# Sparse attention stage: results weighed by branch after the value product, and items turned two behind their scores

## The chip, the cores and the metric

One core of a Trainium2 chip runs the whole program. The metric is device time in microseconds (us). PE is TensorE (PEld its weight loads), DVE is VectorE, ACT is ScalarE, POOL is GpSimd, SP is SyncE, which here only issues DMAs.

## The reference

The program is one layer of a hybrid decoder for a prompt of 1024 tokens and a sample group of 8 sequences with 4 new tokens each and 4096 past tokens. The stage that is changed is the sparse attention (8 heads in 2 key/value groups of 4, head width 64). It computes three attentions per head over the same queries, and adds them with learned gates:

```python
def masked_softmax(s, mask):
    s = jnp.where(mask, s.astype(F32), -1e30)
    m = jnp.max(s, axis=-1, keepdims=True)
    e = jnp.exp(s - m) * mask
    return e / jnp.maximum(jnp.sum(e, axis=-1, keepdims=True), 1e-30)
...
o_c, o_s = nsa_cmp_slc(...)      # compressed blocks of 32 keys; selected blocks of 64 keys
o_w = nsa_window(...)            # the last 512 keys
gt = jax.nn.sigmoid(gl).reshape(Bh, Th, 3, NSA_KV, NSA_GQ, 1)
o = gt[:, :, 0] * o_c + gt[:, :, 1] * o_s + gt[:, :, 2] * o_w
```

The prompt has 16 blocks of 64 keys and 16 are selected, so for the prompt the selected branch is plain causal attention. For the sample group the selection matters, and its keys are gathered by pages of 128 tokens.

## The kernel before

The stage is the function `sparse`. It works through 50 items in one fixed order. 32 of them are prompt items: one of four head pairs (head r of group 0 and head r of group 1, written g = 0, 1) and one tile of 128 queries, tt = 0 to 7. The first head pair takes its tiles in the order 0, 7, 1, 6, 2, 5, 3, 4, the others in the order 0 to 7. From the fifth prompt item on, 18 set items stand between them: a set is one chunk of 512 past keys (4 pages) for 4 sequences of the sample group, 16 of the selected branch and 2 of the window.

A prompt item has a row of scores per query and g: 128(tt+1) columns of the selected branch (SLC), then 128 min(tt+1, 5) of the window (WIN), then 4(tt+1) compressed ones (CMP). It goes through these steps, one after the other, while other items are in the other steps:

- `score` (L1763, PE): the row in chunks of 512 columns, into one of two pairs of PSUM banks (`score_bank`). A chunk waits until DVE has read the chunk two before it (semaphore `biased`).
- `biases` (L2054 to L2061, DVE): adds the bias, writes the row to `s_` (`nsa_probs`, four slots) and takes maxima; from them the negative maxima, which release the exponentials (`negm_ready`).
- `exps` (L1911, ACT): six exponentials in place, one per g and branch, each with its sum.
- `scales` (L2071 to L2080, DVE): from the sums and the gates one factor per query, g and branch, in three small instructions; then six instructions that multiply the row by them.
- `turn` (L1784, PE): transposes blocks of 128 keys, two blocks with both g to a group of one PSUM bank, the compressed keys as a last group. Two such banks are in turn.
- `copies` (L1931, ACT): copies each group to `pt` (`nsa_probs_t`, three slots).
- `values` (L1810, PE): multiplies with the values, two groups behind the turning. All groups of an item add up in one 128 x 128 region of bank 6 or 7.
- `keep_result` (L1949, ACT): copies the region to the output tile.

A set item goes the same way with one chunk (L1752, L2007, L1904), one or two groups (L1777, L1799) and no scaling of its row. The sum of its chunks is formed at the end (L2105, L2108) on DVE.

Each engine's program is written out by hand in steps. In step i PE scores item i and turns item i - LAG, with LAG = 3, chunks of scores and pairs of groups spread evenly among each other (`merged`). ACT in step i copies the groups of item i - 3 and puts one of the six exponentials of item i - 1 before the first and one behind each copy; those that are left come at the end of the step. DVE in step i does `biases(i)` and then `scales(i - 1)`, which has to wait for ACT's last exponential of that item. All engines are in order, so what stands behind a waiting instruction waits as well. In steps 1 and 3 DVE also ranks the blocks of the sample group (`compare`, `count`), and in step 6 it makes masks from the ranks.

SP issues the loads of queries and biases of a head pair (`load`, L1711 and L1714) and of 9 of 16 pages of each set, POOL those of the other 7 (L1702). A set's buffer is free when the values of the set three before it are done. The load of head pair r waits until the last result of head pair r - 2 has been copied out (`o_out`).

Of the kernel before, what the change touches and what calls it, by code (L numbers as in the profile page):

```python
# [13 lines left out]
ALU = mybir.AluOpType  # L14
ACT = mybir.ActivationFunctionType
AX_X = mybir.AxisListType.X
F32 = mybir.dt.float32
# [1527 lines left out]
def sparse(nc, t, u, kv, toeplitz, ident, by_token, out, gdn, spill, kvp, space, pages, kct, vc_past, past_space, early):  # L1545
# [13 lines left out]
    SLOTS, TSLOTS, TBANKS, REGIONS, LAG = 4, 3, 2, 2, 3  # L1559
    PROMPT, SET = range(2)  # L1560
    PAGES, NEWKEYS = "pages", "new"
# [40 lines left out]
    first_chunk, first_group = [0], [0]  # L1602
    for i in range(NI):
        first_chunk.append(first_chunk[-1] + n_chunks(i))
        first_group.append(first_group[-1] + len(groups(i)))
    BEHIND = 2
# [7 lines left out]
    with ExitStack() as ctx:  # L1614
# [12 lines left out]
        assert next_place(nc) - ranking_at >= 3 * 16 * PAGE * 2 and early.end - early.at >= 16 * PAGE * 2  # L1627
# [5 lines left out]
        cnt, flag, addm, near = S("count", [P, IH]), S("flag", [P, NBLK]), S("block_mask", [P, 2, NBLK]), S("near", [P, 2, PAGE])  # L1633
        oc, acc = S("set_out", [P, 2, 2, P]), S("sample_sum", [P, 2, P])
# [4 lines left out]
        def alias(name, shape):  # L1639
# [5 lines left out]
        ring = alias("ring", [P, 2, HB, 4, 2 * PAGE])  # L1645
        third = nc.alloc_sbuf_tensor_at("nsa_ring_third", [P, HB - 1, 4, 2 * PAGE], F32, offset=ranking_at)
        third_last = nc.alloc_sbuf_tensor_at("nsa_ring_third_last", [P, 4, 2 * PAGE], F32, offset=early.at)
# [9 lines left out]
        region = lambda i: ps[:, O_BANK + i % REGIONS, 0:P]  # L1657
        sem = phase_semaphores(ctx, nc, "nsa_")
# [5 lines left out]
        (scores_mm, biased, cleared, max_ready, negm_ready, exp_ready, chain, probs_ready, pt_mm, pt_out, pv_mm, o_mm, o_out) = (  # L1664
            sem(s) for s in ("scores_mm", "biased", "cleared", "max_ready", "negm_ready", "exp_ready", "chain", "probs_ready",
                             "pt_mm", "pt_out", "pv_mm", "o_mm", "o_out"))
# [71 lines left out]
        def _(pe):  # L1738
# [3 lines left out]
            def score(i, c):  # L1742
                kind, n, tt = items[i]
                G = first_chunk[i] + c
# [42 lines left out]
            def values(i, k):  # L1787
# [16 lines left out]
                else:  # L1804
                    for j, (x, col, vb) in enumerate(group):
                        w = 4 * (tt + 1) if x == CMP else P
                        for g in range(2):
# [61 lines left out]
            for i in range(NI + LAG):  # L1869
# [11 lines left out]
                tailing = [(i - LAG, s) for s in range(0, len(groups(i - LAG)), 2)] if i >= LAG else []  # L1881
                for which, (n, k) in merged(scoring, tailing):
                    if which:
# [3 lines left out]
                        values_up_to(first_group[n] + pair[-1] + 1 - BEHIND)  # L1887
                    else:
                        score(n, k)
            values_up_to(first_group[NI])  # L1890
            for hf in range(2):
                pe.wait_ge(sum_ready, hf + 1)
                pe.wait_ge(biased, first_chunk[NI])
# [3 lines left out]
        def _(act):  # L1897
# [43 lines left out]
            def keep_result(i):  # L1941
                kind, n, tt = items[i]
                act.wait_ge(o_mm, i + 1)
                if kind == SET:
                    x, hf, c = sets[n]
                    dst = oc_set[:, hf, c, :] if x == SLC else oc[:, hf, 0, :]
                else:
                    dst = out[:, n, tt * P:(tt + 1) * P]
                act.activation(dst, region(i), ACT.Copy).then_inc(o_out, 1)  # L1949
# [48 lines left out]
        def _(dve):  # L1998
# [13 lines left out]
            def set_biases(i):  # L2012
                x, hf, c = sets[items[i][1]]
                G, dst = first_chunk[i], s_[:, i % SLOTS, 0, :]
# [12 lines left out]
                add_biases(stat_of(items[i][1]), pieces, (biased, first_chunk[i + 1])).then_inc(negm_ready, 1)  # L2027

            def biases(i):
# [12 lines left out]
                for c, pieces in enumerate(chunks(tt)):  # L2042
                    G = first_chunk[i] + c
# [13 lines left out]
                dve.wait_ge(biased, first_chunk[i + 1])  # L2057
# [5 lines left out]
            def scales(i):  # L2063
# [8 lines left out]
                dve.wait_ge(chain, 3 * n + 2)  # L2072
                V.reciprocal(scale[:, p, :, :], scale[:, p, :, :]).then_inc(chain, 1)
                dve.wait_ge(chain, 3 * n + 3)
# [87 lines left out]
            def masks():  # L2162
                dve.wait_ge(spread_mm, 1)
                for hf in range(2):
# [12 lines left out]
            for i in range(NI + 1):  # L2177
# [4 lines left out]
                if i >= 1:  # L2182
                    scales(i - 1)
# [1012 lines left out]
```

## Time and profile before

| | us |
|---|---|
| median of 3 runs (2793.57 to 2802.07) | 2799.81 |
| the profiled execution | 2800.31 |
| its span, first to last instruction | 2798.6 |
| of it the item loop of the sparse stage, 1073.0 to 1440.2 | 367.2 |
| in this stretch: PE busy / DVE busy / ACT busy | 313.1 / 223.4 / 229.3 |

In the whole span PE is busy for 2621.9 us (94%), DVE for 1318.0, ACT for 853.8. The stage stands in slices 16 to 21 of 40, and in them PE has 8s where most other slices have 9s. The stages before and after it do not overlap with it: the first load of the next stage is issued at 1442.64 us and its first matmul starts at 1448.60 us. Times below are from the span's start.

### The profile page before, as it was taken

To read this page: it belongs to the slowest core of one execution; us is meant where nothing else is said; L and a number is where in the kernel's file an instruction comes from. 1 tells how busy PE (TensorE), PEld (TensorE's weight loads), DVE (VectorE), ACT (ScalarE), POOL (GpSimd) and SP (SyncE) were. 2 spreads that over 40 slices of the span, in tenths; PEclk is the share of its full clock that TensorE was granted. 3 is DMA by queue.
4 is the path that set the end of the run, shared out by engine and by line. 5 is a ranking of instruction groups with operands and counts; after the bars stand their busy time and mean duration, and the time that the engine had idled before them with its cause. 6 is when DMAs were issued, how large, how long until landed. Compare 5 with 4: busy or idle time off the path is not lost. (4 is left out here: it accounts for less than half of the span.)

```text
span 2798.6 us, 52706 instructions
## 1 busy us (share of the span) xinstructions
PE 2621.9 (94%) x21842; PEld 2422.9 (87%) x21842; DVE 1318.0 (47%) x2314; ACT 853.8 (31%) x1606; POOL 701.9 (25%) x554
## 2 busy tenths in 40 slices
PE   8999999999889887898879999999999999999997
PEld 7999999999867774555559999988999999999996
DVE  6989999313134357456543453234333323224233
ACT  5323111113123334665642132144221121120222
POOL 2222222222144331212104325201522222222222
PEclk9999999999969898999989999999999999999998
DMA  5122352332287636434335441243111111111111
GB/s 187 46 69 56 105 105 87 93 92 77 95 268 228 205 105 238 150 118 148 104 112 177 137 172 54 68 166 114 46 46 46 46 46 46 46 46 46 46 46 70
DMA packets 149345, 290.33 MB, mean 104 GB/s; under 512 B 28356, under 2 KB 97160, under 8 KB 146354
## 3 DMA queue, kind: packets, MB, share of 16 engines
q1 hardware_dynamic: 137586, 255.49, 28.8%
q0 software_dynamic: 11520, 31.47, 3.6%
q8 instruction: 173, 2.83, 0.4%
q14 instruction: 66, 0.54, 0.1%
HBM read 245.94 MB, written 51.93 MB: 106 GB/s over the span
## 5 line engine op out<-in xcount | busy, mean ns | idle before, releaser
L147 POOL TENSOR_TENSOR mlp_w_low<-mlp_w_raw,mlp_w_high 128x1024 fp32r<-128x1024 f32 x72 | 173.6, 2411 | 649.4 <-ACT mlp_w_high L143 649.4
L373 PE MATMUL in_psum<-x_high,in_w_high 128*128 128x352 f32 x1416 | 265.9, 329 | 21.7 <-DVE x_low L568 11.7
L147 POOL TENSOR_TENSOR in_w_low<-in_w_raw,in_w_high 128x1024 fp32r<-128x1024 f32 x59 | 146.9, 2490 | 547.3 <-ACT in_w_high L143 547.3
L143 ACT ACTIVATE mlp_w_high<-mlp_w_raw 128x1024 fp32r<-128x1024 f32 x72 | 76.4, 1061 | 621.5 <-PE mlp_psum L2850 621.5
L2850 PE MATMUL mlp_psum<-mlp_in,mlp_w_high 128*128 128x352 f32 x1536 | 264.9, 324 | 0.0
L373 PEld LDWEIGHTS in_psum<-x_high,in_w_high 128*128 128x128 f32 x1416 | 236.5, 191 | 29.9 <-issue 15.4
L373 PE MATMUL in_psum<-x_low,in_w_high 128*128 128x352 f32 x1416 | 261.3, 326 | 0.0
L373 PE MATMUL in_psum<-x_high,in_w_low 128*128 128x352 f32 x1416 | 258.7, 324 | 0.0
L2850 PEld LDWEIGHTS mlp_psum<-mlp_in,mlp_w_high 128*128 128x128 f32 x1536 | 251.2, 189 | 0.2
L373 PEld LDWEIGHTS in_psum<-x_low,in_w_high 128*128 128x128 f32 x1416 | 237.4, 191 | 0.0
L373 PEld LDWEIGHTS in_psum<-x_high,in_w_low 128*128 128x128 f32 x1416 | 234.6, 189 | 0.0
L2618 PE MATMUL mix_psum<-branch_halves,mix_w_high 128*128 128x352 f32 x960 | 179.3, 327 | 11.9 <-DVE branch_halves L2703 8.6
L527 DVE SCALAR_TENSOR_TENSOR branches<-glu_prompt,conv_a_taps,branches 128x1024 f32<-128x1024 f32 x120 | 189.6, 1580 | 0.0
L147 POOL TENSOR_TENSOR mix_w_low<-mix_w_raw,mix_w_high 128x1024 fp32r<-128x1024 f32 (+1 forms) x56 | 109.8, 1962 | 306.1 <-ACT mix_w_high L143 306.1
L2850 PE MATMUL mlp_psum<-hidden_high,mlp_w_high 128*128 128x352 f32 x960 | 178.0, 324 | 1.8 <-PEq L86 1.8
L2850 PE MATMUL mlp_psum<-hidden_high,mlp_w_low 128*128 128x352 f32 x960 | 177.8, 324 | 0.0
L2850 PE MATMUL mlp_psum<-hidden_low,mlp_w_high 128*128 128x352 f32 x960 | 177.8, 324 | 0.0
L143 ACT ACTIVATE in_w_high<-in_w_raw 128x1024 fp32r<-128x1024 f32 x59 | 62.4, 1057 | 366.1 <-PE in_psum L373 350.2
L2618 PEld LDWEIGHTS mix_psum<-branch_halves,mix_w_high 128*128 128x128 f32 x960 | 161.0, 191 | 12.6 <-issue 12.4
L2850 PEld LDWEIGHTS mlp_psum<-hidden_high,mlp_w_high 128*128 128x128 f32 x960 | 159.0, 189 | 2.0 <-issue 2.0
L2850 PEld LDWEIGHTS mlp_psum<-hidden_high,mlp_w_low 128*128 128x128 f32 x960 | 159.2, 189 | 0.0
L2850 PEld LDWEIGHTS mlp_psum<-hidden_low,mlp_w_high 128*128 128x128 f32 x960 | 159.0, 189 | 0.0
(493 smaller groups left out, 4429.8 us busy)
## 6 DMA issues: line engine op xcount, KB each, us to landing
mlp_w_raw<-in_w_mlp SPq DMA_DIRECT2D x64, 512.0 KB, 3.6
in_w_raw<-in_w_in SPq DMA_DIRECT2D x59, 512.0 KB, 4.2
gdnp_page_ring<-in_cache_cmp POOLq DMA_DIRECT2D x128, 128.0 KB, 4.8
gdnp_page_ring<-in_cache_cmp SPq DMA_DIRECT2D x128, 128.0 KB, 4.9
u_scratch<-stage SPq DMA_DIRECT2D x28, 528.0 KB, 5.2
aux<-u_scratch SPq DMA_DIRECT2D x24, 528.0 KB, 4.0
nsa_ring<-in_cache_slc SPq DMA_DIRECT2D x90, 128.0 KB, 4.0
nsa_ring<-in_cache_slc POOLq DMA_DIRECT2D x70, 128.0 KB, 4.1
```

What stands on the lines that cost most here:

```text
L143: act.activation(self.high[:, i % 2, 0:k * P], self.raw[:, i % 2, 0:k * P], ACT.Copy).then_inc(self.rounded, 1)
L147: self.nc.gpsimd.tensor_tensor(self.low[:, i % 2, 0:k * P], self.raw[:, i % 2, 0:k * P], self.high[:, i % 2, 0:k * P].bitcast(F32), ALU.su ...
L373: return mm(psum[:, e % 2, n, 0:WN], w[:, i % 2, c * P:(c + 1) * P], a[:, c, n * WN:(n + 1) * WN], start=x == 0 and c == 0, stop=x == 2 an ...
L527: V.scalar_tensor_tensor(out=y, in0=src, scalar=w, in1=y, op0=ALU.mult, op1=ALU.add).then_inc(conv_chain, 1)
L2618: return mm(psum[:, e % 2, n, 0:cols.stop - cols.start], w[:, i % 2, c * P:(c + 1) * P], a(c)[:, cols], start=x == 0 and c == 0, stop=x == ...
L2850: return mm(psum[:, e % 2, n, 0:WN], w[:, i % 2, c * P:(c + 1) * P], a(c)[:, column(n)], start=x == 0 and c == 0, stop=x == 2 and c == CHU ...
```

## The change

The row of exponentials is no longer multiplied. The values are multiplied with the bare exponentials, each branch into a region of its own (three of 128 columns in the same bank). The three factors per query and g are brought into the layout of the result by six small matmuls per prompt item (`factors`: the factor column, repeated 64 times, as weights, against the identity), which take the place of one chunk in the score banks. ACT copies all three regions (384 columns in place of 128) to `weighed`; DVE multiplies them with the factors and adds the three (`combine`). DVE computes the factors three steps after the item's biases instead of one, and combines in the fourth step after. LAG is 2 in place of 3, so PE turns and ACT copies an item one step sooner; turning waits for the exponentials alone. The load of head pair r waits for the maxima of the last item of head pair r - 2 (`negm_ready`) instead of its result. To find room, some small tiles of the sample group (`near`, `addm`, `acc`) lie in memory that is free by then, and the masks wait for the end of one early store (`spilled`).

```diff
-    SLOTS, TSLOTS, TBANKS, REGIONS, LAG = 4, 3, 2, 2, 3
+    SLOTS, TSLOTS, TBANKS, REGIONS, LAG = 4, 3, 2, 2, 2
...
-    first_chunk, first_group = [0], [0]
+    of_step = lambda step: step - LAG - 2
+    STEPS = NI + LAG + 2
+    combined = lambda step: of_step(step) >= 0 and items[of_step(step)][0] == PROMPT
+    chunk_at, factors_at, n_all_chunks, first_group = [], {}, 0, [0]
+    for step in range(STEPS):
+        chunk_at.append(n_all_chunks)
+        n_all_chunks += n_chunks(step) if step < NI else 0
+        if combined(step):
+            factors_at[step] = n_all_chunks
+            n_all_chunks += 1
...
-    BEHIND = 2
+    BEHIND, BEFORE_SCALES = 2, 3
...
+        by_branch = lambda i: ps[:, O_BANK + i % REGIONS, 0:3 * P].rearrange("p (x n) -> p x n", x=3)
...
                 if r >= 2:
-                    sp.wait_ge(o_out, last_of_head[r - 2] + 1)
+                    sp.wait_ge(negm_ready, last_of_head[r - 2] + 1)
...
+            def factors(step):
+                G, n = factors_at[step], prompts_before[of_step(step)]
+                if G >= 2:
+                    pe.wait_ge(biased, G - 1)
+                pe.wait_ge(scale_ready, n + 1)
+                for x in range(3):
+                    for g in range(2):
+                        last = mm(score_bank(G, 0)[g * DH:(g + 1) * DH, x * P:(x + 1) * P],
+                                  scale[:, n % SLOTS, g, x:x + 1].to_broadcast([P, DH]), ident[:, :], start=True, stop=True)
+                last.then_inc(scores_mm, 1)
...
                 if k == 0:
-                    pe.wait_ge(*((probs_ready, prompts_before[i + 1]) if kind == PROMPT else (exp_ready, i + 1)))
+                    pe.wait_ge(exp_ready, i + 1)
...
-                            last = mm(region(i)[dims, :], v, pt[0:w, G % TSLOTS, 2 * j + g, :], start=k == 0 and j == 0, stop=x == CMP)
+                            last = mm(by_branch(i)[dims, x, :], v, pt[0:w, G % TSLOTS, 2 * j + g, :], start=vb == first_block,
+                                      stop=x == CMP or vb == tt)
...
                 scoring = [(i, c) for c in range(n_chunks(i))] if i < NI else []
-                tailing = [(i - LAG, s) for s in range(0, len(groups(i - LAG)), 2)] if i >= LAG else []
+                if i in factors_at:
+                    scoring.append((i, FACTORS))
+                tailing = [(i - LAG, s) for s in range(0, len(groups(i - LAG)), 2)] if LAG <= i < NI + LAG else []
+                if i == NI + LAG:
+                    values_up_to(first_group[NI])
...
-                    dst = out[:, n, tt * P:(tt + 1) * P]
-                act.activation(dst, region(i), ACT.Copy).then_inc(o_out, 1)
+                before = prompts_before[i]
+                if before >= 2:
+                    act.wait_ge(prompt_out, before - 1)
+                act.activation(weighed[:, before % 2, :, :], by_branch(i), ACT.Copy).then_inc(o_out, 1)
...
-                V.tensor_tensor(scale[:, p, :, :], scale[:, p, :, :], gate, ALU.mult).then_inc(chain, 1)
-                dve.wait_ge(chain, 3 * n + 4)
-                for g in range(2):
-                    for x, at, w in spans(tt):
-                        src = s_[:, i % SLOTS, g, at:at + w]
-                        last = V.tensor_scalar(src, src, scale[:, p, g, x:x + 1], None, ALU.mult)
-                last.then_inc(probs_ready, 1)
+                V.tensor_tensor(scale[:, p, :, :], scale[:, p, :, :], gate, ALU.mult).then_inc(scale_ready, 1)
+
+            def combine(step):
+                m = of_step(step)
+                kind, r, tt = items[m]
+                G, n = factors_at[step], prompts_before[m]
+                dve.wait_ge(scores_mm, G + 1)
+                dve.wait_ge(o_out, m + 1)
+                rows = weighed[:, n % 2, :, :]
+                V.tensor_tensor(rows, rows, score_bank(G, 0)[:, 0:3 * P].rearrange("p (x n) -> p x n", x=3), ALU.mult).then_inc(biased, 1)
+                dve.wait_ge(biased, G + 1)
+                V.tensor_reduce(out[:, r, tt * P:(tt + 1) * P], rows.rearrange("p x n -> p n x"), AX_X, ALU.add
+                                ).then_inc(prompt_out, 1)
...
             def masks():
                 dve.wait_ge(spread_mm, 1)
+                dve.wait_ge(spilled, 16)
...
-            for i in range(NI + 1):
+            for i in range(STEPS):
                 if i == RANKED:
                     masks()
                 if i < NI:
                     biases(i)
-                if i >= 1:
-                    scales(i - 1)
+                if BEFORE_SCALES <= i < NI + BEFORE_SCALES:
+                    scales(i - BEFORE_SCALES)
+                if i in factors_at:
+                    combine(i)
```

## Rows read from the trace of the kernel before

**Rows 1.** Busy time and PEclk by stretch: the item loop, then two shorter stretches.
```profile
core 0: us, PE busy (x) PEld busy (x) DVE busy (x) ACT busy (x) POOL busy (x), PEclk, DMA share, GB/s
1073.00:1440.20 367.20, 313.07 (x3115) 202.04 (x3115) 223.35 (x1035) 229.33 (x666) 61.13 (x112) 0.93 0.39 128
1265.00:1275.00 10.00, 6.41 (x54) 4.12 (x52) 6.64 (x39) 2.86 (x10) 0.00 (x0) 0.68 0.58 206
1320.00:1335.00 15.00, 12.96 (x140) 8.38 (x136) 9.66 (x38) 10.31 (x27) 4.12 (x7) 1.00 0.44 142
```

**Rows 2.** Waits in the item loop: us in total, times, longest.
```profile
PE nsa_psum L1763 <- DVE nsa_part_max L2054: 34.0, 22, 8.7
PE nsa_psum L1784 <- ACT nsa_probs_t L1931: 6.9, 14, 1.1
PE nsa_psum L1752 <- DMA nsa_ring_third<-in_cache_slc: 6.6, 1, 6.6
PE nsa_psum L1784 <- DVE nsa_probs L2080: 5.5, 7, 2.0
...
DVE nsa_scale L2071 <- ACT nsa_probs L1911: 34.3, 20, 3.5
...
ACT nsa_probs L1911 <- DVE nsa_negmax L2061: 63.7, 27, 6.4
```

**Rows 3.** Timeline around one stall: start, duration, instruction, idle before it.
```profile
1300.36 0.17 DVE L2071 TENSOR_SCALAR nsa_scale<-nsa_sums 128x6 f32<-128x6 f32 x1 [2.83 <-ACT nsa_probs L1911]
...
1301.00 2.23 DVE L2080 TENSOR_SCALAR nsa_probs<-nsa_probs,nsa_scale 128x640 f32<-128x640 f32 x6
...
1304.49 0.92 PE L1763 MATMUL nsa_psum<-nsa_k_prompt,nsa_q_heads 64*128 64x384 f32 x4 [1.99 <-DVE nsa_part_max L2054]
...
1307.43 0.94 ACT L1911 ACTIVATE nsa_probs<-nsa_probs,nsa_negmax 128x768 f32<-128x768 f32 x1 [4.88 <-DVE nsa_negmax L2061]
```

**Rows 4.** Groups by line, the stage: form, count, busy us, mean ns, idle before.
```profile
L2080 DVE TENSOR_SCALAR nsa_probs<-nsa_probs,nsa_scale 128x640 f32<-128x640 f32 (+11 forms) x192 | 64.1, 406 | 1.1
L1810 PE MATMUL nsa_psum<-nsa_probs_t,nsa_v_by_token 128*64 128x128 f32 x1056 | 78.7, 284 | 0.0
L1949 ACT ACTIVATE branches<-nsa_psum 128x128 f32<-128x128 f32 x32 | 8.4, 264 | 1.1 <-PE nsa_psum L1810 0.9
```

**Rows 5.** PE in the timeline at full clock: scores, transposes, values, a set's scores.
```profile
1412.35 1.13 PE L1763 MATMUL nsa_psum<-nsa_k_prompt,nsa_q_heads 64*128 64x512 f32 x4
1434.24 1.09 PE L1810 MATMUL nsa_psum<-nsa_probs_t,nsa_v_by_token 128*64 128x128 f32 x16
1431.22 1.09 PE L1784 MATMUL nsa_psum<-ident,nsa_probs 128*128 128x128 f32 x8
1259.72 1.06 PE L1752 MATMUL nsa_psum<-nsa_ring,early_q_padded 128*32 128x512 f32 x8
```

**Rows 6.** Groups by line with shapes kept apart: the nearest forms to what is added.
```profile
L2007 DVE CUSTOM_DVE_ANT_1 nsa_probs<-nsa_psum,nsa_block_mask 128x384 f32<-128x384 f32 x2 | 1.1, 554 | 2.2 <-PE nsa_psum L1752 2.2
L1931 ACT ACTIVATE nsa_probs_t<-nsa_psum 128x512 f32<-128x512 f32 x146 | 86.0, 591 | 59.4 <-PE nsa_psum L1784 38.6 <-PE nsa_psum L1777 9.8 <-PE nsa_psum L1810 7.6
L1931 ACT ACTIVATE nsa_probs_t<-nsa_psum 128x256 f32<-128x256 f32 x8 | 3.1, 383 | 2.2 <-PE nsa_psum L1784 1.7 <-PE nsa_psum L1810 0.3
```

**Rows 7.** Timeline of the loop's start: exponentials of item 1, a reduction, PE's return.
```profile
1080.67 1.15 ACT L1911 ACTIVATE nsa_probs<-nsa_probs,nsa_negmax 128x1024 f32<-128x1024 f32 x1 [2.70 <-DVE nsa_negmax L2061]
...
1082.19 0.28 DVE L2146 TENSOR_REDUCE nsa_score<-nsa_psum 128x64 f32<-128x128 f32 x1
...
1085.09 0.19 ACT L1911 ACTIVATION_READ_ACCUMULATOR nsa_probs<-nsa_probs,nsa_negmax 128x1 f32 x1
...
1089.53 3.78 PE L1763 MATMUL nsa_psum<-nsa_k_prompt,nsa_q_heads 64*128 64x512 f32 x12 [8.70 <-DVE nsa_part_max L2054]
```

**Rows 8.** Timeline: SP's queue at the load of a head pair.
```profile
1170.33 0.33 SPq L1711 DMA_DIRECT2D nsa_q_heads<-u_scratch  x1
```

**Rows 9.** Timeline of the loop's end: ACT's last copies.
```profile
1440.00 1.61 ACT L1994 ACTIVATE branches<-nsa_psum 64x16 f32<-64x16 f32 x16
```

More of the change, by code:

```diff
@@ L1558, in sparse @@
     CMP, SLC, WIN = range(3)
-    SLOTS, TSLOTS, TBANKS, REGIONS, LAG = 4, 3, 2, 2, 3
+    SLOTS, TSLOTS, TBANKS, REGIONS, LAG = 4, 3, 2, 2, 2
     PROMPT, SET = range(2)
-    PAGES, NEWKEYS = "pages", "new"
+    PAGES, NEWKEYS, FACTORS = "pages", "new", "factors"
     sets = [(x, hf, c) for hf in range(2) for x, c in [(WIN, 0)] + [(SLC, c) for c in range(NCH)]]
@@ L1626, in sparse @@
         lower, gtm, eqm = (sb(ctx, nc, "nsa_" + n, [P, IH, NBLK], dt) for n, dt in (("lower", U16), ("greater", BF16), ("equal", BF16)))
-        assert next_place(nc) - ranking_at >= 3 * 16 * PAGE * 2 and early.end - early.at >= 16 * PAGE * 2
+        assert next_place(nc) - ranking_at >= 3 * 16 * PAGE * 2 + 8 * NBLK and early.end - early.at >= 16 * PAGE * 2
         gates24, gates = S("gates24", [P, 2, 3, NSA_HEADS]), S("gates", [P, 2, 3])
@@ L1632, in sparse @@
         inv, score, scol = S("inv", [P, 2]), S("score", [P, NBLK]), S("score_col", [P, IH])
-        cnt, flag, addm, near = S("count", [P, IH]), S("flag", [P, NBLK]), S("block_mask", [P, 2, NBLK]), S("near", [P, 2, PAGE])
-        oc, acc = S("set_out", [P, 2, 2, P]), S("sample_sum", [P, 2, P])
+        cnt, flag = S("count", [P, IH]), S("flag", [P, NBLK])
+        oc, weighed = S("set_out", [P, 2, 2, P]), S("weighed", [P, 2, 3, P])
+        assert NCMP == P
+        acc = sc
         least, weight, total, coef = S("least", [P, 2]), S("weight", [P, 2, NCH]), S("total", [P, 2, NCH + 4]), S("coef", [P, 2, NCH + 2])
@@ L1645, in sparse @@
         ring = alias("ring", [P, 2, HB, 4, 2 * PAGE])
+        near = alias("near", [P, 2, PAGE])
+        assert place[0] <= space + 2 * 4 * 4 * W
         third = nc.alloc_sbuf_tensor_at("nsa_ring_third", [P, HB - 1, 4, 2 * PAGE], F32, offset=ranking_at)
+        addm = nc.alloc_sbuf_tensor_at("nsa_block_mask", [P, 2, NBLK], F32, offset=ranking_at + 3 * 16 * PAGE * 2)
         third_last = nc.alloc_sbuf_tensor_at("nsa_ring_third_last", [P, 4, 2 * PAGE], F32, offset=early.at)
@@ L1663, in sparse @@
             "k_in", "v_turned", "v_ready", "vc_turned", "vc_ready", "spilled"))
-        (scores_mm, biased, cleared, max_ready, negm_ready, exp_ready, chain, probs_ready, pt_mm, pt_out, pv_mm, o_mm, o_out) = (
-            sem(s) for s in ("scores_mm", "biased", "cleared", "max_ready", "negm_ready", "exp_ready", "chain", "probs_ready",
-                             "pt_mm", "pt_out", "pv_mm", "o_mm", "o_out"))
+        (scores_mm, biased, cleared, max_ready, negm_ready, exp_ready, chain, scale_ready, pt_mm, pt_out, pv_mm, o_mm, o_out, prompt_out) = (
+            sem(s) for s in ("scores_mm", "biased", "cleared", "max_ready", "negm_ready", "exp_ready", "chain", "scale_ready",
+                             "pt_mm", "pt_out", "pv_mm", "o_mm", "o_out", "prompt_out"))
         (lower_in, zeroed, bias_mm, bias_ready, m0_mm, m0_read, turned_mm, turned, past_mm,
@@ L1743, in score @@
                 kind, n, tt = items[i]
-                G = first_chunk[i] + c
+                G = chunk_at[i] + c
                 if G >= 2:
@@ L1806, in values @@
                         w = 4 * (tt + 1) if x == CMP else P
+                        first_block = {SLC: 0, WIN: max(0, tt - 4), CMP: 0}[x]
                         for g in range(2):
@@ L1868, in _ @@
             pe.wait_ge(k_in, 32)
-            for i in range(NI + LAG):
+            for i in range(STEPS):
                 if i == LAG:
@@ L1887, in _ @@
                         values_up_to(first_group[n] + pair[-1] + 1 - BEHIND)
+                    elif k == FACTORS:
+                        factors(n)
                     else:
                         score(n, k)
-            values_up_to(first_group[NI])
             for hf in range(2):
                 pe.wait_ge(sum_ready, hf + 1)
-                pe.wait_ge(biased, first_chunk[NI])
+                pe.wait_ge(biased, n_all_chunks)
                 tr(ps[:, hf, 0:P], acc[:, hf, :], ident[:, :]).then_inc(final_mm, 1)
@@ L2026, in set_biases @@
                         pieces += [(dst[:, at:BANK], src[:, at:BANK], near[:, hf, :]), new(1)]
-                add_biases(stat_of(items[i][1]), pieces, (biased, first_chunk[i + 1])).then_inc(negm_ready, 1)
+                add_biases(stat_of(items[i][1]), pieces, (biased, chunk_at[i] + 1)).then_inc(negm_ready, 1)
             def biases(i):
@@ L2176, in _ @@
             dve.wait_ge(chain, 1)
-            for i in range(NI + 1):
+            for i in range(STEPS):
                 if i == RANKED:
```

15 lines of the change are left out of this document (7 added, 8 removed).

## The prediction, made before the changed kernel was run

> **What bounds the kernel now.** I read the waits first, then stretches of the stage, then one stall in the timeline. The item loop lasts 367.2 us; PE is busy for 313.1 of them, DVE for 223.4 and ACT for 229.3 [rows 1]. So PE is the fullest engine, but it stands for 54.1 us, and it also works slowly at times: the mean granted clock is 0.93, which is 313.1 x 0.07 = 22 us of its busy time. What does it wait for? 34.0 us for DVE's reading of a score bank, 5.5 for DVE's scaling of a row, 6.9 for ACT's copies of turned groups, 6.6 once for a page load [rows 2]. DVE is no full engine either. It stands for 34.3 us until ACT has done an item's last exponential, and ACT stands for 63.7 us until DVE has the next item's negative maxima [rows 2]. That is a ring: `scales(i - 1)` waits for the exponentials of i - 1, `biases(i + 1)` stands behind it on DVE, PE's score chunks and ACT's next exponentials wait for that. One turn of it in the timeline [rows 3]: DVE stands 2.83 us for ACT, multiplies for 2.23 us, reads banks again, PE comes back after 1.99 us of idling and ACT after 4.88. The clock follows such stalls: in 1265 to 1275, with PE busy for 6.41 of 10 us, it is 0.68, so for much of the stretch the engine ran at 1.2 GHz instead of 2.4; in 1320 to 1335, busy for 12.96 of 15 us with many small gaps, it is 1.00 [rows 1].
>
> **The change part by part.**
>
> 1. Six multiplications per prompt item go from DVE: 192 instructions, 64.1 us [rows 4]. The three small instructions before them stay, but two steps later, when the exponentials are long done, so DVE's 34.3 us of waiting goes with them.
>
> 2. DVE gets two instructions per prompt item. The product reads 384 columns from PSUM: the nearest row is a bias addition of that size from PSUM, 554 ns [rows 6]. The sum reads 384 and writes 128 columns, in steps of 128 columns. The nearest row is a reduction of 128 columns, 0.28 us; at about 1.05 ns per column (0.55 - 0.28 us over 256 columns) 384 columns make 0.55 us [rows 6, 7]. From both sides: 0.28 us if its size cost nothing, 1.1 us if the stride doubled it. Together 32 x 1.1 = 35 us. DVE's load falls from 223 to about 194 us of the loop, and the 29 us are worth nothing by themselves, since DVE isn't the fullest engine. If the stride cost double, DVE would still be at 212.
>
> 3. PE gets six matmuls per prompt item, on the path. Their shape is that of the value products: weights 128 x 64, 128 columns moving, the two g in different halves of the array. The trace records each value product twice (528 products, 1056 records), and 16 records take 1.03 us from one group's start to the next one's [rows 4, 5]. 12 records are 0.77 us, over 32 items **25 us**. Below: 0.27 us less per item if the weights, one repeated column, loaded free (about 16 us in all). Above: 50 us if the two g didn't run side by side. I take 25, since the form is the row's own.
>
> 4. ACT's copy of a result grows from 128 to 384 columns: from 264 ns to a value between 383 (256 columns) and 591 (512), about 487 [rows 4, 6]. 32 x 0.22 = 7 us, beside PE's work; ACT then has about 236 of the loop.
>
> 5. The ring is cut, so PE's 34.0 + 5.5 us lose their cause. What is late next? With LAG = 2 PE turns item i - 2 in step i, and ACT did its exponentials in step i - 1, at that step's end where the copies beside them are few. To size it I wrote down, for each step, what each engine has to do. PE: 0.25 us + 2.2 ns per column of score width, 0.54 us per block of 128 keys (four records of 64 ns for its two value products, two transposes of 136 ns) and once more for the compressed keys, 0.17 us per group; a set 1.1 + 1.9 us [rows 5]. ACT: per exponential 0.27 us + 0.86 ns per column (1.15 us for 1024 columns, 4.6 for the six of item 1 [rows 7]), 0.6 us per full group, the result. DVE: 0.09 us + 1.04 ns per column, and the small instructions. For the kernel before, with LAG = 3, these sums give PE 326, ACT 243 and DVE 223 us, close to the trace. If each step lasts as long as its fullest engine, the loop is 363 us, that is 37 over PE's sum; measured are 54.1 - 6.6 (the load) = 47.5 of idling. For the kernel after they give PE 350, ACT 250, DVE 191 and 370 in all, 20 over PE's sum: 7 in steps 0 and 1, where DVE ranks, and 13 in ten steps where ACT is the fullest, most of them with a set's single group. An example is step 24: ACT copies a set's group and does the six exponentials of a tile with tt = 7 (4.6 + 0.9 us), while PE has the scores of a tile with tt = 0, the set's tail, and no factors (0.8 + 1.9 us). Scaled with what the sums missed before, 20 x 47.5 / 37 = **25 us** of idling after.
>
> 6. The start. PE stands for 8.70 us until 1089.53, while DVE ranks [rows 7]. With LAG = 2 it can turn item 0 in step 2; item 1 it can turn once its exponentials end at about 1085.3 [rows 7]. This is part of the 25 us.
>
> 7. Loads. PE waited 6.6 us for pages of the third buffer [rows 2]; SP had issued a head pair's load at 1170.33, just ahead of them [rows 8]. A set's buffer comes free one step (some 7 us) sooner, and the head pair's load may go four steps sooner, so I count this wait as gone; if it stays, 6.6 us come back. On SP's queue the load keeps its place in the order, and the page loads behind it wait for later values anyway. POOL's queue loses nothing.
>
> 8. The clock. Before, 22 us go to slow stretches, and they follow the longer stalls [rows 1]. With idling about halved I halve this: 12 us. The range is 5 to 22.
>
> 9. The end. Two more of the small tails: PE does the last two items' factors (counted), ACT's last copy is 0.22 us longer, and DVE's 1.1 us run beside the 1.61 us of ACT's last copies [rows 9]. 0.5 us. The new waits of `masks` for a store and of ACT for `prompt_out` are for work done steps before; I see nothing to be late there, and cost them at nothing. If the second were late, copies would stand behind it and PE would show it as waits for `nsa_probs_t`.
>
> The sum: 313.1 - 22 = 291 us of PE's work at full clock, + 25 (factors), + 25 (idling), + 12 (clock), + 0.5 = 353.5, against 367.2: 13.7 us less. All other stages keep their time, since the next one starts its loads only when this one is over. The profiled execution took 2800.3 us, which is 0.5 above the median of the runs; 2800.3 - 13.7 = **2786.6 us**.
>
> **A rule that speaks against step 8.** In the item loop PE had many gaps under 1 us with the clock at 1.00, as in 1320 to 1335 [rows 1]. The Trainium skill, page "TensorE: Matmul & The Clock Gate", section "A second HAM failure mode: psum-queue depth-cycling", says that frequent short gaps between groups of matmuls, as banks are cycled, are enough to make the clock swing. By that rule the changed loop, with more and shorter waits, keeps its 22 us. The trace disagrees so far.
>
> **The rivals.**
>
> *Clock and waits stay (same time).* The gaps are shared out differently, but the clock loss stays at 22 us and idling falls only to 36 (the sums' 20 + the 16 by which measured idling exceeds them at the start and in ping-pong between PE and ACT). 291 + 25 + 36 + 22 = 374 is 7 over; with either alone it is 363 to 364, about 4 less. So 2796 to 2807, centre 2800. For it: ACT's share rises and its copies already cost PE 6.9 us [rows 2]. Against: DVE's 34 us have no other cause than the ring. A clock that alone stays as it was gives the 363.
>
> *The exponentials are late (slower).* Place: the first `turn` of a step. 30 of 50 items are followed into it by an item with four groups or fewer (18 sets, 12 tiles with tt up to 2), where ACT has up to four of six exponentials left behind its last copy: two thirds of 4.6 us for the widest. PE covers this with its last two groups of values, the factors and one score chunk, together up to 1.1 + 0.8 + 1.1 us [rows 5]. It decides from the point where the exponentials left over take longer than that cover. If the cover is mostly only the values, about 1.6 us are lost each time, 48 us, and with the clock at its old loss: 291 + 25 + 22 + 48 = 386, that is 19 over, 2819 us.
>
> *The factors cost double (slower).* If the repeated column as weights keeps the two g from running side by side, 25 more: 2812 us. It would show at once in the group of the new line.
>
> *More is gained (faster).* If idling falls to 15 us and the clock loss to 5, the loop is 336 and the time 2769. For it: PE can be nearly gapless, 14.6 of 15 us, where nothing but turning and values is left; but that is without scores, so I give it little.
>
> *The change doesn't do what it says*, that is, DVE still waits for ACT or PE in `combine`: the factors stand last in a step, and DVE waits for them with the next `biases` behind it. But those need scores that PE issues later still, so this wait costs nothing by itself.
>
> **How the numbers follow.** Forecast (2779 to 2796) 0.48; same 0.20; exponentials late 0.12; factors double 0.06; more gained 0.14. The predicted time is the forecast's, 2787. The range 2768 to 2811 takes in the forecast, the same, the gain and most of the doubled factors, and leaves out the late exponentials and the tails. What a measurement of this kernel can tell from no change is about 0.3%, 8.4 us, so faster means under 2791.4: 0.36 of the forecast's 0.48 and the 0.14, together 0.50. Same: the remaining 0.12 and 0.19 of the same, 0.31. Slower: 0.19.
>
> **What would show it right or wrong.** Right: the group of the multiplications is gone; DVE's wait for ACT is near 0 and PE's for DVE's reading is under 10 us, most of it at the start; the new matmuls come to about 25 us in 384 records; PE's wait for pages is gone; PEclk in the loop is 0.96 or more. Wrong: transposes that wait for `nsa_probs` of ACT for more than 20 us (exponentials late), a new line's group near 50 us (factors), a clock that stays at 0.93.

## The result, and the profile after

The changed kernel takes 2805.95 us (median of 20 runs, 2794.79 to 2813.06), the kernel before, measured beside it, 2795.9 us (20 runs). The ratio is 1.0031, with a 95% interval of 1.0021 to 1.0040: it is slower by 0.3%, at the edge of what can be told from no change. The prediction was 2787 us, faster. The time lies within the range, on the wrong side of no change.

The same view as [rows 1], for the item loop of the kernel after, cut at two instructions, its first score matmul and PE's last transpose:

```profile
core 0: us, PE busy (x) PEld busy (x) DVE busy (x) ACT busy (x) POOL busy (x), PEclk, DMA share, GB/s
1081.32:1450.69 369.37, 330.82 (x3499) 225.40 (x3498) 197.23 (x907) 241.66 (x664) 60.31 (x112) 0.94 0.38 124
```

The loop of the kernel before, cut at the same two instructions:

```profile
1073.20:1440.07 366.87, 312.87 (x3115) 201.97 (x3114) 223.35 (x1035) 229.20 (x664) 61.13 (x112) 0.93 0.39 128
```

The waits of the kernel after, as in [rows 2] (engine, tile and line, what it waited for: us in total, times, longest):

```profile
DVE nsa_weighed L2118 <- PE nsa_psum L1788: 39.1, 24, 6.2
...
PE nsa_psum L1809 <- ACT nsa_probs L1943: 27.6, 19, 3.5
...
PE nsa_psum L1777 <- DVE nsa_part_max L2088: 3.7, 3, 2.8
...
PE nsa_psum L1788 <- DVE nsa_part_max L2088: 2.1, 1, 2.1
PE nsa_psum L1777 <- DVE nsa_score L2186: 2.0, 1, 2.0
```

The new groups, as in [rows 4, 6]:

```profile
L1788 PE MATMUL nsa_psum<-ident,nsa_scale 128*64 128x128 f32 x384 | 26.6, 275 | 2.1 <-DVE nsa_part_max L2088 2.1
...
L2120 DVE TENSOR_REDUCE branches<-nsa_weighed 128x128 f32<-128x384 f32 x32 | 19.0, 594 | 1.1
L2118 DVE TENSOR_TENSOR nsa_weighed<-nsa_weighed,nsa_psum 128x384 f32<-128x384 f32 x32 | 17.7, 554 | 44.4 <-PE nsa_psum L1788 39.1 <-issue 5.1
L1983 ACT ACTIVATE nsa_weighed<-nsa_psum 128x384 f32<-128x384 f32 x32 | 15.4, 483 | 3.7 <-PE nsa_psum L1836 3.7
```

The reader should see three things. The ring of [rows 2, 3] is gone: DVE no longer waits for an exponential, PE's 34.0 us for the reading of a bank before its scores are 3.7 (and 2.1 before the factors), and the wait for pages isn't there. A new wait has come: 19 times PE stands before a transpose (L1809) until ACT has done the exponentials (L1943), 27.6 us. And PEclk is 0.94, where 0.96 or more was expected.

The profiled run of after took 2810.4 us, and most of its difference from before's profiled run lies ahead of the loop: the loop started at 1081.32 instead of 1073.20, and stages ahead of it, which the change doesn't touch, had a lower granted clock in that execution. A second profile, below, has no such difference. So parts are compared here by the length of the loop.

### The profile page after: what moved, and what is told of

It reads as the page before. It is cut to its first block and busy times, and to the rows that moved or that the text cites. A ratio compares the mean times of both kernels' runs of the same rounds, so it can differ in the third digit from the quotient of the medians.

```text
span 2808.7 us, 53440 instructions
## 1 busy us (share of the span) xinstructions
PE 2648.5 (94%) x22226; PEld 2453.9 (87%) x22226; DVE 1293.6 (46%) x2186; ACT 867.0 (31%) x1606; POOL 702.3 (25%) x554
## 5 line engine op out<-in xcount | busy, mean ns | idle before, releaser
L373 PE MATMUL in_psum<-x_high,in_w_high 128*128 128x352 f32 x1416 | 265.9, 329 | 21.9 <-DVE x_low L568 11.9
L2661 PEld LDWEIGHTS mix_psum<-branch_halves,mix_w_high 128*128 128x128 f32 x960 | 160.7, 191 | 12.4 <-issue 12.2
```

The source lines that it names most:

```text
L373: return mm(psum[:, e % 2, n, 0:WN], w[:, i % 2, c * P:(c + 1) * P], a[:, c, n * WN:(n + 1) * WN], start=x == 0 and c == 0, stop=x == 2 an ...
L2661: return mm(psum[:, e % 2, n, 0:cols.stop - cols.start], w[:, i % 2, c * P:(c + 1) * P], a(c)[:, cols], start=x == 0 and c == 0, stop=x == ...
```

## The experiments

Each loop was cut at the same instructions. From its row I work out three shares: idling is its length less PE's busy time, the clock's part is busy time x (1 - PEclk), and work at full clock is the rest. PEclk has two digits, so the last two shares are good to about 1.7 us. Each row is one profiled execution; the ratio is that of the timed runs, by their medians. All in us, but for the ratio:

| kernel | loop | idling | clock | work | ratio to before, 95% interval |
|---|---|---|---|---|---|
| before | 366.9 | 54.0 | 21.9 | 291.0 | |
| after, first profile | 369.4 | 38.6 | 19.8 | 311.0 | 1.0031 [1.0021, 1.0040] |
| after, second profile | 374.1 | 38.8 | 23.5 | 311.8 | 1.0033 [1.0021, 1.0045] |
| after with LAG 3 | 337.8 | 19.8 | 9.5 | 308.4 | 0.9901 [0.9886, 0.9916] |
| after, exponentials first | 346.8 | 27.7 | 6.4 | 312.7 | 0.9955 [0.9940, 0.9969] |
| LAG 3, exponentials first | 336.0 | 22.1 | 3.1 | 310.8 | 0.9901 [0.9879, 0.9922] |
| LAG 3, one third of the factors | 326.3 | 24.2 | 6.0 | 296.1 | 0.9862 [0.9841, 0.9884] |
| LAG 3, factors twice | 355.9 | 17.7 | 6.8 | 331.5 | 0.9960 [0.9944, 0.9977] |
| LAG 3, the old load | 345.9 | 26.1 | 9.6 | 310.2 | 0.9919 [0.9889, 0.9949] |
| before with LAG 2 | 472.7 | 121.9 | 63.1 | 287.7 | 1.0389 [1.0366, 1.0412] |
| before, factors an item later | 431.5 | 92.5 | 47.5 | 291.5 | 1.0242 [1.0228, 1.0256] |
| before, factors ahead of the biases | 367.5 | 51.1 | 25.3 | 291.1 | 0.9995 [0.9979, 1.0010] |

**The changed kernel again.** No edit.

> The changed kernel once more, unaltered, for a second profile. In the first one the item loop took 369.6 us (before: 367.2), while the stages ahead of it had taken 5.3 us more and the prelude of the sparse stage 2.8 us more, both at a lower granted clock. Theory A (these 8 us are what the clock does from run to run, and the loop's 2 to 3 us are the change): the loop again takes 367 to 372 us, and the time ahead of the loop differs from 1081 us, towards 1073. Rival (the change reaches the stages ahead of it, through where tiles or code lie): the loop starts again at 1080 us or later.

2805.94 us. The loop starts at 1072.16, close to before's 1073.20, and lasts 374.1 us:

```profile
1072.16:1446.26 374.10, 335.27 (x3498) 227.75 (x3498) 197.41 (x907) 241.86 (x664) 60.11 (x112) 0.93 0.38 126
```

So the later start of the first profile was not the change. The loss inside the loop is 7.2 us here and 2.5 in the first profile. The wait for exponentials is the same to 0.1 us (27.6, 19 times, longest 3.5). What differs between the two profiles is mostly the clock: 3.7 of the 4.7 us.

**LAG 3 again.** Of the change the weighing by branch and the earlier load of the head pairs stay, so this is not the weighing alone, as the expectation calls it.

```diff
-    SLOTS, TSLOTS, TBANKS, REGIONS, LAG = 4, 3, 2, 2, 2
+    SLOTS, TSLOTS, TBANKS, REGIONS, LAG = 4, 3, 2, 2, 3
```

> The changed kernel with LAG = 3, so items are turned three behind their scores as before, and only the weighing by branch is left of the change. Theory A (the 27.6 us that PE waits for ACT's exponentials come from turning an item sooner; the 26.6 us of factor matmuls stay): that wait falls under 3 us, the loop to 367.2 + 26.6 - (34.0 + 5.5 + most of the 6.6) - some clock = 345 to 352 us, and the time to 2778 to 2785 us. Rival B (ACT's copies and exponentials hold PE up whatever the lag; the waits turn up as waits for nsa_probs_t or for banks): the loop stays within 3 us of 369.6 and the time at 2800 to 2806.

2768.51 us, more than was expected, and better than both kernels. Its loop row:

```profile
1072.58:1410.33 337.75, 317.95 (x3499) 215.17 (x3498) 195.97 (x907) 235.44 (x665) 60.11 (x112) 0.97 0.42 137
```

The same stretch in two parts, split after the first 37 us:

```profile
1072.58:1109.58 37.00, 27.24 (x211) 17.31 (x210) 28.78 (x120) 21.39 (x68) 7.55 (x14) 0.82 0.74 254
1109.58:1410.33 300.75, 290.71 (x3292) 197.87 (x3288) 167.19 (x787) 214.05 (x599) 52.56 (x98) 0.99 0.38 123
```

The largest waits of PE in it (L1777 is the scores, L1788 the factors, L1809 the turning):

```profile
PE nsa_psum L1777 <- DVE nsa_part_max L2088: 10.0, 6, 7.0
PE nsa_psum L1809 <- ACT nsa_probs_t L1963: 5.8, 11, 1.4
PE nsa_psum L1788 <- DVE nsa_part_max L2088: 1.6, 4, 0.4
```

Turned three items behind, no transpose waits for an exponential. After the first 37 us PE idles for 10.0 of 300.75 us. Against before the loop is 29.1 us shorter: 34.2 less idling and 12.4 less to the clock, for 17.4 more work. LAG 2 then takes 36.3 back (second profile): 19.0 of idling, 14.0 of clock, and 3.4 of work, which is within what two digits of PEclk allow. The change is two changes of opposite sign.

**The exponentials ahead of the copies** (after, LAG 2). ACT puts as many of the six before its first copy as would be left behind the last one.

```diff
-                next(exp_parts, None)
+                for _ in range(max(1, 6 - len(groups(i)))):
+                    next(exp_parts, None)
```

> The changed kernel, LAG = 2, with ACT's order altered in steps with fewer than five groups: the exponentials that were left behind the last copy are done ahead of the first one. Theory A says that PE's 27.6 us are these leftovers: the wait for them halves at least (under 14 us), the loop falls by 5 to 15 us to 355 to 365. Rival B: the copies are late instead and PE waits as long for nsa_probs_t or its values; the loop stays at 366 to 372 us.

2782.22 us. The wait falls from 27.6 to 10.7 us, the loop by 27.3 against the second profile, of which 11.1 are idling and 17.1 the clock. Its loop row:

```profile
1072.14:1418.93 346.79, 319.05 (x3499) 217.48 (x3498) 197.26 (x907) 238.91 (x665) 60.11 (x112) 0.98 0.42 134
```

And what is left of PE's wait:

```profile
PE nsa_psum L1809 <- ACT nsa_probs L1943: 10.7, 10, 2.9
PE nsa_psum L1809 <- ACT nsa_probs_t L1964: 5.8, 8, 1.4
```

The second line is new: with copies standing behind exponentials, 5.8 us of the 16.9 come back as waits for copies, which is why idling falls by 11.1 only. The loops behind their first 37 us, of the second profile of the changed kernel and then of this one:

```profile
1109.16:1446.26 337.10, 306.45 (x3278) 208.97 (x3274) 168.86 (x793) 219.25 (x598) 52.80 (x99) 0.93 0.35 112
1109.14:1418.93 309.79, 290.24 (x3278) 198.66 (x3274) 168.80 (x793) 216.02 (x596) 52.57 (x99) 0.99 0.39 122
```

Nothing but ACT's order was changed, so the late exponentials are shown as the cause of the waits, and the clock's loss goes with them. The profiled execution was the fastest of six (2778.05 us); by the medians the gain is 23.7 us and not 27, so the typical clock loss is some us above the 6.4 of the table.

**The same order with LAG 3.** Both edits.

> by_branch_lag3 with the order of exponentials of exps_first. With LAG = 3 no one waits for the exponentials any more. Theory A: no gain, the loop stays at 337.8 +- 3 us and the time at 2766 to 2771. Rival B (ACT's order also delays copies with LAG = 3, and the 5.8 us that PE waits for nsa_probs_t go up): 341 us or more.

2768.94 us, no different from LAG 3 alone. Where the exponentials have a step to spare, their place costs nothing.

**Before with LAG 2.**

```diff
-    SLOTS, TSLOTS, TBANKS, REGIONS, LAG = 4, 3, 2, 2, 3
+    SLOTS, TSLOTS, TBANKS, REGIONS, LAG = 4, 3, 2, 2, 2
```

> The kernel before with LAG = 2 and nothing else: the other half of the change alone. Theory A (turning an item sooner has no slack for the steps between scores and turning; here these are the exponentials and also DVE's multiplications): PE waits for nsa_probs of DVE or ACT for far more than the 27.6 us of the changed kernel, 40 to 80 us, and the loop of 367 us grows to 395 to 430, the time to 2825 to 2860. Rival B (the lag by itself costs little, and only the two together meet): the loop stays under 380 us.

2906.61 us, far worse than I thought: with the row still to be multiplied, exponentials, factors and products all have to be done in the slack that is left. PE's largest wait, for the multiplied rows (L2080):

```profile
PE nsa_psum L1784 <- DVE nsa_probs L2080: 113.8, 28, 7.7
```

So the rest of the change, without which LAG 2 costs 3.9%, brings it to 0.3%, but doesn't make it free.

**Before, with the factors an item later.** DVE multiplies the row of item i - 2 behind the biases of item i.

```diff
-                if i >= 1:
-                    scales(i - 1)
+                if i >= 2:
+                    scales(i - 2)
```

> The kernel before, with the whole row still multiplied on DVE, but one step later: scales(i - 2) behind biases(i). No factor matmuls, LAG = 3. Theory A (the ring between DVE and ACT was the whole of the stall, and it can be cut without any work on PE): DVE's wait of 34.3 us for the exponentials falls under 8 us, PE's 34.0 us for score banks under 15, the loop to 335 to 350 us and the time to 2768 to 2783. Rival B: PE's first turn of a step now waits for the multiplications, which end after the biases of that step; 50 steps x 1 us or more come back as waits for nsa_probs of DVE, the loop stays at 360 us or more.

2866.46 us, a miss. The wait of DVE for exponentials goes from 34.3 to 1.0 us, as meant, but the multiplied rows now come late for PE:

```profile
PE nsa_psum L1784 <- DVE nsa_probs L2080: 77.6, 29, 5.1
```

At this place the multiplication cuts the ring and misses another due time, that of the turning. No other place was tried that differs from the kernel before (the next experiment does not), so what is shown is that taking it out of the row's path pays and this move doesn't.

**Before, with the factors ahead of the biases.** The same call, put ahead of `biases(i)`.

> The kernel before with the row multiplied on DVE at the start of the next step: scales(i - 2) ahead of biases(i) instead of scales(i - 1) behind biases(i). scales_later (behind biases(i)) had cut DVE's wait for the exponentials to 1.0 us, but PE waited 77.6 us for the multiplied rows and the loop took 431 us. Theory A (with LAG = 3 there is one step for it: done first, the rows are ready when PE turns them; DVE waits a little for the last exponentials, PE a little for banks): loop 345 to 365 us. Rival B (DVE's multiplications stand between the scores of a step and the maxima that ACT waits for, wherever they are put, so the ring is there again): 365 us or more, with PE's wait for score banks at 30 us or more.

2795.01 us, no difference. The experiment was badly chosen: biases i, factors i - 1, biases i + 1 is the very order of the kernel before, only cut into steps elsewhere. DVE waits for exponentials for 29.9 us (18 times), PE for the reading for 30.8. It says nothing on either theory, except that the place of the ranking beside these calls doesn't matter.

**A third of the factor matmuls** (LAG 3).

```diff
-                for x in range(3):
+                for x in range(1):
```

> by_branch_lag3 with two of the six factor matmuls per item (one branch of three), 128 in place of 384 records; the product then reads what lies in the banks for the other two branches, so the prompt's attention result isn't computed fully. It prices the matmuls on PE's path. Theory A (PE is the engine that sets the pace, and each record costs its 64 to 70 ns): the loop falls by two thirds of 26.6, 17 to 18 us, from 337.8 to about 320, the time from 2768.5 to 2750 to 2753. Rival B (the matmuls lie partly in gaps of PE): it falls by less than 9 us.

2758.85 us. The kernel leaves out the factors of two of the three branches, so it serves as a price only. PE works 15.8 us less and the loop is 11.4 shorter (9.7 by the medians), between the two expectations: 72% of the time taken away counts. The rest turns into idling (24.2 in place of 19.8).

**The factor matmuls twice** (LAG 3).

```diff
-                for x in range(3):
+                for x in (0, 1, 2, 0, 1, 2):
```

> As by_branch_lag3, with the six factor matmuls issued twice per prompt item (12; the second six write the same values again). The attention result is complete. by_branch_lag3 had 2768.5 us, a loop of 337.8 and 26.6 us in the factor matmuls; with two of six left it had 9.7 us less for 15.8 us less of PE work. Theory A, the matmuls lie on the path where PE is the fullest engine and in PE's idle time elsewhere, so some 65 to 90% of their time counts: the added 26 us make the loop 17 to 25 us longer (355 to 363), 2785 to 2794 us, and PE's busy time in the loop rises to about 343. Rival B, they are fully on the path, or worse (the first bank's clock loss grows): 26 us or more, 2795 or above. Rival C, mostly hidden beside the chunk's waits: under 12 us, below 2781.

2789.32 us. PE works 20.3 us more, the loop is 18.2 longer: 90%. Little of the added work finds cover. The group of the factors' line in this kernel:

```profile
L1788 PE MATMUL nsa_psum<-ident,nsa_scale 128*64 128x128 f32 x768 | 48.8, 278 | 1.7 <-DVE nsa_part_max L2088 1.6
```

And with the plain LAG 3, so that twice the matmuls take 21.2 us more, 0.66 per item:

```profile
L1788 PE MATMUL nsa_psum<-ident,nsa_scale 128*64 128x128 f32 x384 | 27.6, 281 | 1.7 <-DVE nsa_part_max L2088 1.6
```

**The old load** (LAG 3).

```diff
-                    sp.wait_ge(negm_ready, last_of_head[r - 2] + 1)
+                    sp.wait_ge(o_out, last_of_head[r - 2] + 1)
```

> As by_branch_lag3, with the load of head pair r waiting again for the last result of head pair r - 2, as in the kernel before, in place of its maxima. It prices that part of the change. Theory A: the head pair's load is issued some four steps later, and the page loads that stand behind it in SP's queue with it, so a wait of PE for pages comes back, once, of 3 to 8 us, and the time is 2771 to 2777. Rival B: the page loads wait for their buffers anyway and nothing in the time changes, 2767 to 2770, with the set's scores waiting under 1 us for pages.

2777.34 us; the loop is 8.2 us longer, and by the two ratios the difference is 5 us (0.0018 x 2797), with intervals that overlap. The wait of [rows 2] is back in its old place:

```profile
PE nsa_psum L1766 <- DMA nsa_ring_third<-in_cache_slc: 6.3, 1, 6.3
```

What SP waited for, with the old load and then with the new one:

```profile
SPq L1725 <- ACT nsa_weighed L1983: 16.1, 1, 16.1
SPq L1716 <- PE nsa_psum L1824: 10.3, 1, 10.3
```

SP's queue in the timeline, with the old load:

```profile
1171.13 0.33 SPq L1725 DMA_DIRECT2D nsa_q_heads<-u_scratch  x1
...
1177.08 1.39 SPq L1716 DMA_DIRECT2D nsa_ring_third<-in_cache_slc  x3
```

The same with the new load:

```profile
1153.57 0.43 SPq L1725 DMA_DIRECT2D nsa_q_heads<-u_scratch  x1
...
1170.30 1.39 SPq L1716 DMA_DIRECT2D nsa_ring_third<-in_cache_slc  x3
```

With the old load SP stood for 16.1 us until ACT had copied a result (L1983), and the page loads stood behind it. With the new one SP gets to them in time and waits only for their buffer (L1824, 10.3 us). The pages are issued 97.7 us after the loop's start in place of 103.4.

## Why the prediction was wrong, step by step

Predicted for the loop were 316 us of PE's work at full clock with the factors, 25 of idling, 12 of clock and 0.5 at the end. Measured in the first profile were 311.0, 38.6 and 19.8. So 13.6 us were missed in idling and 7.8 in the clock, and 5.5 were counted too much in work and the end: together 15.9, which is 369.4 - 353.5. In the second profile the loop is 20.6 us over the forecast. By the medians of the runs 13.7 us less were forecast and 10.1 more came.

1. *The multiplications and DVE's wait*: right. Both are gone.
2. *DVE's two instructions*: right, 554 + 594 ns for 0.55 + 0.55 us. The sum, with its stride, takes 594 ns, near the 0.55 said and far from 1.1. DVE is busy for 197 us (194 said). Its 39.1 us of waiting for the factors' matmuls in `combine` cost nothing that shows: with exponentials first they are 39.9 and the loop is 27 us shorter.
3. *The factors*: right in size, 26.6 us for 25 in 384 records, where two g one behind the other would have made 50. The work at full clock rose by less, 20.0 and 20.8 us. With LAG 3, 72 to 90% of a change in their time counts.
4. *ACT's copy*: right, 483 ns for 487.
5. *What is late next*: **this step failed.** The forecast put 16 us (13 in ten steps, scaled) on steps in which ACT is the fullest engine; the trace has 27.6 in 19 places, since what decides is not which engine is fullest but whether the exponentials end before the next step's first transpose. The prediction's example, step 24, in the changed kernel's timeline:

```profile
1249.89 0.72 PE L1777 MATMUL nsa_psum<-nsa_k_prompt,nsa_q_heads 64*128 64x128 f32 x8
...
1250.65 0.66 PE L1802 MATMUL nsa_psum<-ident,nsa_probs 128*128 128x128 f32 x4
...
1251.24 0.66 PE L1836 MATMUL nsa_psum<-nsa_probs_t,nsa_v_by_token 128*64 128x128 f32 x8
...
1255.35 1.97 PE L1809 MATMUL nsa_psum<-ident,nsa_probs 128*128 128x128 f32 x8 [3.46 <-ACT nsa_probs L1943]
...
1257.87 1.94 PE L1824 MATMUL nsa_psum<-nsa_ring,nsa_probs_t 128*32 128x128 f32 x32
```

The example gave 5.5 us of ACT against 2.7 of PE, so 2.8; PE stands for 3.46. Its 2.7 us held the set's values (L1824), but these come behind the transpose that waits. What PE has to cover the exponentials with ends at 1251.9, after 2.0 us. The same in step 37, where ACT again has a set's group and the exponentials of a tile with tt = 7, and PE also a set's scores and the factors:

```profile
1342.79 0.82 PE L1788 MATMUL nsa_psum<-ident,nsa_scale 128*64 128x128 f32 x12
...
1345.15 0.81 ACT L1943 ACTIVATE nsa_probs<-nsa_probs,nsa_negmax 128x640 f32<-128x640 f32 x1
...
1346.17 0.19 ACT L1943 ACTIVATION_READ_ACCUMULATOR nsa_probs<-nsa_probs,nsa_negmax 128x1 f32 x1
...
1346.41 1.09 PE L1809 MATMUL nsa_psum<-ident,nsa_probs 128*128 128x128 f32 x8 [2.80 <-ACT nsa_probs L1943]
```

PE ends the factors at about 1343.6 and stands for 2.80 us until ACT's last exponential; by the prediction's prices the step has 5.5 us of ACT and 3.8 of PE, so 1.7. All 13 waits of over 1 us, 25.2 us together, stand behind a step in which a set is turned. An estimate with the prediction's own prices: in ten of the 19 steps PE has more to do than ACT, and they hold 13 of the 27.6 us; the sum of the fullest engine counts nothing there. The other nine hold 14.6, where the sums give about 10.

The sums ask only whether an engine has more to do in a step than the others. But ACT's copies wait for transposes of the same step, the exponentials that are left over come behind the last copy, and the last of them has to be there before the next step's first transpose: with LAG 2 that is a due time within the step, which a step can miss though ACT is not its fullest engine. The run with the exponentials first bears this out: ACT had the same work in each step, and 17 of the 27.6 us went. The scaling by 47.5 / 37 couldn't find this, since it was taken from a kernel with LAG 3, in which that due time has a step of slack.

The rival "the exponentials are late" had the place, and nearly the size of one (1.6 us, measured 27.6 / 19 = 1.45), but put it at 30 places instead of 19; I held it for a separate case with 0.12, while part of it was already in the forecast. Its sign, over 20 us of such waits, came; its 2819 us did not. What came, by numbers, is the rival "clock and waits stay": 36 of idling and 22 of clock were said there, 38.7 and 21.7 are the means of the two profiles, and 2800 us was its centre. That is luck: its cause was shared-out small gaps and not the exponentials, and its 36 was 20 + 16, where the 16 follows from neither of the prediction's differences (54.1 - 37 = 17.1, 47.5 - 37 = 10.5).

6. *The start*: right. PE's waits for DVE there are 3.7 + 2.1 + 2.0 = 7.8 us, 7 said.
7. *Loads*: the wait is gone. A buffer that comes free a step sooner isn't needed for it: with LAG 3 moving the head pair's load is enough. Behind the new load the page loads do wait for values, as said (10.3 us); behind the old one the load itself held them back. In the loops this part is worth 8.2 us, 6.3 of them the wait for pages; by the medians it is about 5, with intervals that overlap.
8. *The clock*: **this step failed too**, as a consequence. 19.8 and 23.5 us were lost, where 12 were said. With LAG 3 the 9.5 are below my 12. That half the idling means half the loss had no ground: with exponentials first idling is 27.7, half of before's 54.0, and the clock's part 6.4. By the rule of the Trainium skill, page "TensorE: Matmul & The Clock Gate", section "A second HAM failure mode: psum-queue depth-cycling", the loss would stay, and it did in the changed kernel. But with LAG 3 and the same matmuls in the same banks the clock is 0.99 after the first 37 us, so it isn't the cycling of banks with short gaps that holds it down here. In both profiles of the changed kernel, behind the first 37 us, every four microseconds with a granted clock under 0.97 lie at a stall of 1.5 to 3.5 us or in the ten us behind one.
9. *The end*: nothing to be seen there. From the next stage's first load to the end it is 1355.4 us after and 1356.0 before.

The larger miss in method: I costed LAG 3 to 2 only as a part of the whole, never by itself. The ring is cut without LAG 2. What LAG 2 adds, once the ring is cut, is a buffer freed a step sooner, which PE never had to wait for with LAG 3, and 37 us of loss by the medians.

## What to carry to other kernels

Where a change has two parts, forecast each alone, with the other as it was: here one gained 28 us by the medians (about 5 of them from the earlier load) and the other lost 37. In a software pipeline a lag is slack for whatever stands between two engines; before shortening it, list for each step what has to be finished before the step's first dependent instruction, and not only which engine is fullest. If the lag must be short, put the instructions that the other engine waits for first: that gave back 24 of the 37 us.

## What the runs showed of the hardware

The same stall doesn't always cost the same clock. The two profiles of the changed kernel have the same waits for exponentials, each of those over 1 us to 0.02 us, but a transpose group of eight records takes 1.09 us at the full clock (2.4 GHz) and 1.97 where the granted clock is at its lower level (1.2 GHz), and after equal stalls one profile shows the first and the other the second. From the timeline of the first profile:

```profile
1158.67 1.09 PE L1809 MATMUL nsa_psum<-ident,nsa_probs 128*128 128x128 f32 x8 [2.24 <-ACT nsa_probs L1943]
...
1215.49 1.09 PE L1809 MATMUL nsa_psum<-ident,nsa_probs 128*128 128x128 f32 x8 [2.14 <-ACT nsa_probs L1943]
```

The second profile, the same two places in the timeline:

```profile
1148.56 1.97 PE L1809 MATMUL nsa_psum<-ident,nsa_probs 128*128 128x128 f32 x8 [2.25 <-ACT nsa_probs L1943]
...
1206.82 1.97 PE L1809 MATMUL nsa_psum<-ident,nsa_probs 128*128 128x128 f32 x8 [2.13 <-ACT nsa_probs L1943]
```

At the second place the first profile has no drop at all, its PEclk is 1.00 for the ten us behind the stall. At the first place it has one that comes later: PEclk is 0.50 from 1160.67 to 1162.67. After the 2.80 us at 1346.41 the transposes still ran fast, and the next four microseconds were slow with PE busy all the time. Three stretches of the first profile, with the columns of the loop's row:

```profile
1344.00:1348.00 4.00, 1.59 (x12) 1.15 (x12) 0.81 (x2) 3.66 (x11) 0.00 (x0) 0.93 0.00 0
1348.00:1352.00 4.00, 4.00 (x50) 3.44 (x49) 0.44 (x5) 1.26 (x3) 1.23 (x3) 0.50 0.17 49
1352.00:1356.00 4.00, 4.00 (x34) 3.33 (x35) 1.02 (x13) 1.79 (x3) 2.54 (x5) 0.72 0.97 313
```

So a stall of 1.5 to 3.5 us costs itself and, often, slower microseconds behind it; why the clock falls in one execution and not in the other stays open. Most of the difference between the loops of one and the same kernel, 369.4 and 374.1 us, is this. The time ahead of the loop differed by 8 and 9 us between executions (from 1000 us to the loop's start PEclk was 0.83 in the slowest of them and 0.91 in the other two); why stays open. A difference of a few microseconds has to be read from the loop's parts, not from the span.
